# Sixteen more tokens by gathered rows: a dense expert product of 368 columns in place of 384

## The chip, the cores and the metric

The kernel runs on one core of one Trainium2 chip. The metric is the device time of one execution in microseconds, and lower is better. Engines are named as in the profile: PE (TensorE matmul), PEld (its weight loads), DVE (VectorE), ACT (ScalarE), POOL (GpSimd), and SP, which only issues DMAs.

## The reference

One encoder layer over 512 tokens of width 2048. Token mixers come first. What matters here is the last part, a product-key expert layer: each token picks 8 x 16 = 128 of 16384 single-neuron experts, each with a gate, and the output is

```
a   = u_sel . x                      # first expert product
hid = gelu(a) * gate
out = sum over the 128 experts of hid * v_sel   # second expert product
x   = x + out ; out = rmsnorm(x) * g_final
```

## The kernel before

Tokens lie on the free dimension, 512 columns. The first expert product is dense: gelu(u x) for all 16384 experts is written to a DRAM scratch, `act_dram` (128 tiles of 128 experts x 512 tokens). The second product is done in two ways at once in the last stage, the value stage.

**Dense part, 384 tokens (`TD`).** POOL scatter-adds the gates of these tokens into `gates_dram` (L705). The value stage runs over 16 sub-blocks `s` of eight tiles, and each sub-block over 16 output tiles `x`. One (s, x) is called a half here: 256 halves. A half takes one 512 KB piece of `w_v` in a ring of four slots. ACT rounds it (`round_half`, L752: `w_hi`), POOL subtracts (L738: `w_lo`), and PE does 8 x 3 matmuls with `TD` columns (L2079 to L2081): hi x hi, hi x lo, lo x hi. SP loads a slot again once its `w_lo` is made, ACT rounds once PE is done with the half four earlier. DVE adds the result into `yv` (L2053). For eight of the 16 tiles (`PREPARED_AT` = 0, 2, 4, ... 12, 13) the engines also prepare the operand of the next sub-block: DVE multiplies gelu by gate (`product`, L1996), ACT rounds it (`hidden`, L1189) and issues the next loads, DVE subtracts (`low_part`, L2000). ACT does `hidden` ahead of the `round_half` of the same x.

**Gathered part, the last 128 tokens.** One token per partition. For each of its 128 experts POOL issues an indirect DMA that gathers 128 gelu values (`gather_act`, L720) and one that gathers 128 rows of `v_rows`, 1 MB (`gather_row`, L730). DVE multiplies the row by the token's factor and adds it to `y_sparse` in four PSUM banks (`add_row`, L2032). Three row buffers (`ROW_BUFS`). In sub-block 15 ACT copies the sums out, PE turns them (L2459), and DVE adds them to `yv` (L2049).

**The order is written out by hand.** POOL's value loop has a step q for each half: `w_lo` of half q+4, then what `GATHERS[q]` holds. DVE adds the rows of step q at half q+3 (`ROW_LAG`), behind the add of that half and ahead of the product of the next. Before the change, steps 1 to 32 have one act gather each, and from 33 on two steps of every three have an act gather (up to step 175) and, from 36 to 226, the same two of three have a row gather.

## Time and profile before

| what | us |
|---|---|
| median of 3 runs (4304.68 to 4309.94) | 4307.83 |
| profiled execution, its own time | 4316.3 |
| its span | 4314.5 |
| PE busy | 4238.6 |
| POOL busy | 2527.8 |
| DVE busy | 2519.5 |
| ACT busy | 1573.2 |

Matmuls overlap, so PE's busy time says that it had work and not how fast it went; the spacing of matmuls comes from counting them in a window. Idle time in brackets stands in front of an instruction, with what ended it. POOL's row for an indirect DMA is the time in which it makes the DMA, not the transfer. "issue" is time that no wait in the profile explains.

### The profile page before, as it was taken

The page shows a single profiled execution, that of the slowest core. Times are in us where ns is not written, and L with a number is a line of the kernel's source. Part 1 is how long each engine was busy: PE and PEld are TensorE (multiplying, and loading weights), DVE is VectorE, ACT ScalarE, POOL GpSimd, SP SyncE. Part 2 cuts the span into 40 slices and gives each one's busy share as a digit, 9 for nine tenths or more (in the row PEclk, how much of TensorE's full clock was granted, in tenths as well). Part 3 has the DMA queues.
Part 4 walks back from the last instruction along what each step waited for, and adds up shares of the span by engine and source line. Part 5 has one row for each costly group of instructions (what it writes and reads, how often), then busy time and mean ns, then how long its engine had stood idle before and what let it go on. Part 6 is the DMA issues. An engine that isn't in the chain of part 4 may idle for free.

```text
span 4314.5 us, 67486 instructions
## 1 busy us (share of the span) xinstructions
PE 4238.6 (98%) x24940; PEld 3881.5 (90%) x24940; DVE 2519.5 (58%) x3662; ACT 1573.2 (36%) x2079; POOL 2527.8 (59%) x1276
## 2 busy tenths in 40 slices
PE   7999999999999999999999999999989999999998
PEld 6888888888887877888899999999989999999998
DVE  5422443445545433896577777777762477777655
ACT  5222333333334433222444444444443333322332
POOL 5333344443443444444588888887018888888774
PEclk9999999999999999999999999999999999999999
DMA  6696566666667873233355555555465899999983
GB/s 246 198 386 184 153 209 190 186 190 187 183 197 235 268 223 119 93 100 121 113 129 133 125 136 132 129 132 129 137 208 178 282 331 337 333 337 335 356 299 112
DMA packets 574119, 870.50 MB, mean 202 GB/s; under 512 B 85648, under 2 KB 423952, under 8 KB 556944
## 3 DMA queue, kind: packets, MB, share of 16 engines
q1 hardware_dynamic: 401536, 591.47, 43.1%
q0 software_dynamic: 77824, 134.52, 11.8%
q10 hardware_dynamic: 94608, 142.52, 9.3%
q8 instruction: 92, 1.51, 0.1%
q14 instruction: 59, 0.48, 0.0%
HBM read 784.55 MB, written 218.04 MB: 232 GB/s over the span
## 4 chain that ended last, share of the span: by engine, by line
PE 75%; issue 10%; POOL 8%; DMA 3%; DVE 2%; ACT 1%; ACTq 0%; POOLq 0%; DVEq 0%; SPq 0%
PE banks L2079 17%; PE banks L2081 17%; PE banks L2080 17%; PE banks L2416 7%; PE banks L2417 7%; PE banks L2415 7%; POOL w_lo L682 4%; POOL w_lo L738 3%; DMA arena<-expert_rows_scratch,constants 2%; POOL constants L720 1%; PE banks L2280 1%; POOL arena L730 1%; DVE arena L1393 0%; DMA constants<-gelu_scratch 0%; PE banks L2375 0%
## 5 line engine op out<-in xcount | busy, mean ns | idle before, releaser
L2079 PE MATMUL banks<-x_hi,w_hi 128*128 128x512 f32 (+1 forms) x4800 | 1776.4, 370 | 32.4 <-DVE x_lo L2000 15.8
L2080 PE MATMUL banks<-x_lo,w_hi 128*128 128x512 f32 (+2 forms) x4928 | 1798.1, 365 | 0.0
L2081 PE MATMUL banks<-x_hi,w_lo 128*128 128x512 f32 (+1 forms) x4800 | 1761.2, 367 | 0.0
L682 POOL TENSOR_TENSOR w_lo<-w_raw,w_hi 128x1024 fp32r<-128x1024 f32 x364 | 898.7, 2471 | 1425.2 <-ACT w_hi L752 1222.4
L2079 PEld LDWEIGHTS banks<-x_hi,w_hi 128*128 128x128 f32 x4800 | 904.9, 189 | 147.1 <-DVE x_lo L2000 13.3
L2080 PEld LDWEIGHTS banks<-x_lo,w_hi 128*128 128x128 f32 x4928 | 931.5, 189 | 104.4 <-issue 1.2
L752 ACT ACTIVATE w_hi<-w_raw 128x1024 fp32r<-128x1024 f32 x612 | 643.4, 1058 | 1015.2 <-PE banks L2081 909.1
L2081 PEld LDWEIGHTS banks<-x_hi,w_lo 128*128 128x128 f32 x4800 | 904.4, 188 | 108.9
L705 POOL DMA_INDIRECT gate_matrix_scratch<-arena,constants x384 | 741.4, 1931 | 116.9 <-issue 116.9
L738 POOL TENSOR_TENSOR w_lo<-w_raw,w_hi 128x1024 fp32r<-128x1024 f32 x252 | 609.0, 2426 | 142.2 <-ACT w_hi L752 137.9
L2417 PE MATMUL banks<-x_hi,w_lo 128*128 128x256 f32 x1664 | 470.8, 283 | 0.0
L2416 PE MATMUL banks<-x_lo,w_hi 128*128 128x256 f32 x1664 | 470.7, 283 | 0.0
L2415 PE MATMUL banks<-x_hi,w_hi 128*128 128x256 f32 x1664 | 470.6, 283 | 0.0
L2032 DVE SCALAR_TENSOR_TENSOR banks<-arena,constants,banks 128x2048 f32<-128x2048 f32 x127 | 298.8, 2353 | 142.3 <-DMA arena<-expert_rows_scratch,constants 136.0
L2417 PE MATMUL banks<-t_hi,w_lo 128*128 128x256 f32 x1248 | 350.4, 281 | 0.0
L2415 PE MATMUL banks<-t_hi,w_hi 128*128 128x256 f32 x1248 | 350.1, 281 | 0.0
L2416 PE MATMUL banks<-t_lo,w_hi 128*128 128x256 f32 x1248 | 349.9, 280 | 0.0
L2416 PEld LDWEIGHTS banks<-x_lo,w_hi 128*128 128x128 f32 x1664 | 316.2, 190 | 0.0
L2417 PEld LDWEIGHTS banks<-x_hi,w_lo 128*128 128x128 f32 x1664 | 316.2, 190 | 0.0
L2415 PEld LDWEIGHTS banks<-x_hi,w_hi 128*128 128x128 f32 x1664 | 316.0, 190 | 0.0
L2053 DVE TENSOR_TENSOR arena<-arena,banks 128x384 f32<-128x384 f32 x256 | 139.6, 549 | 245.6 <-PE banks L2081 201.2
L1927 DVE TENSOR_TENSOR w_lo<-w_raw,w_hi 128x1024 fp32r<-128x1024 f32 x156 | 190.3, 1220 | 81.3 <-ACT w_hi L1149 81.2
(291 smaller groups left out, 4546.9 us busy)
## 6 DMA issues: line engine op xcount, KB each, us to landing
expert_rows_scratch<-w_v SPq DMA_DIRECT2D x256, 512.0 KB, 5.1
w_raw<-w_u SPq DMA_DIRECT2D x256, 512.0 KB
w_raw<-w_v SPq DMA_DIRECT2D x256, 512.0 KB
w_raw<-w_in SPq DMA_DIRECT2D x200, 512.0 KB
gelu_scratch<-arena ACTq DMA_DIRECT2D x126, 256.0 KB
gate_matrix_scratch<-early_mix_or_one_hots SPq DMA_DIRECT2D x16, 1536.0 KB, 9.6
constants<-gelu_scratch ACTq DMA_DIRECT2D x128, 192.0 KB
early_mix_or_one_hots<-gate_matrix_scratch ACTq DMA_DIRECT2D x32, 768.0 KB
```

What stands on the lines that cost most here:

```text
L682: nc.gpsimd.tensor_tensor(wlo[s][:], raw[s][:], whi[s][:], ALU.subtract).then_inc(w_lo_made, 1)
L705: nc.gpsimd.indirect_dma_start(gate_values, bass.IndirectOffsetOnAxis(gate_index[:, tt, e:e + 1], 0), sel[:, 2, tt, e:e + 1], None, comput ...
L738: nc.gpsimd.tensor_tensor(wlo[m % 4][:], raw[m % 4][:], whi[m % 4][:], ALU.subtract)\
L752: A.activation(whi[s][:], raw[s][:], ACT.Copy).then_inc(w_hi_made, 1)
L1927: V.tensor_tensor(wlo[s][:], operand_source(name), whi[s][:], ALU.subtract).then_inc(pair_lo, 1)
L2032: V.scalar_tensor_tensor(y_sparse, rows[:, e % ROW_BUFS], hid_sparse[:, e:e + 1], y_sparse, ALU.mult, ALU.add).then_inc(rows_added, 1)
L2079: M.matmul(out, whi[s][:, k], h, start=f, stop=False)
L2080: M.matmul(out, whi[s][:, k], l, start=False, stop=False)
L2081: ins = M.matmul(out, wlo[s][:, k], h, start=False, stop=e)
L2415: M.matmul(out, whi[s][:, k], h, start=k == 0, stop=False)
L2416: M.matmul(out, whi[s][:, k], l, start=False, stop=False)
L2417: ins = M.matmul(out, wlo[s][:, k], h, start=False, stop=k == HT - 1)
```

## The change

Sixteen of the 384 dense tokens (the last of them) move to the gathered way. As they are few, each gets eight partitions: partition 8t+g handles 16 of token t's 128 experts. So 16 more act gathers and 16 more row gathers (`E_SLOTS`) are issued, and go through the same row buffers and the same `y_sparse` ahead of the other tokens. DVE then copies the sums to SBUF (`extra_sums`), and PE adds the eight partitions of each token by 16 small products with `group_ones` in sub-block 14. Index values are spread over the partitions through a small DRAM scratch, by DMAs from POOL ahead of the value stage. Dense operands, matmuls, loads and adds have 368 columns (`TV`). Act gathers are now in three of four steps (12 to 181), row gathers in two of three (13 to 227), in blocks of 16 (`HID_BLOCK`) for the factors.

```diff
@@ -70,9 +70,13 @@
 TD = T - P
+EXTRA = 16
+TV = TD - EXTRA
+E_GROUPS = P // EXTRA
+E_SLOTS = P // E_GROUPS
 TG = TD // P
 NE = NK * NK
-HID_BLOCK = 32
+HID_BLOCK = 16
 ROW_BUFS = 3
@@ -162,10 +166,12 @@
     at = {}
+    for j in range(E_SLOTS):
+        at.setdefault((2 * j) // 3, []).append(("extra_act", j))
     for e in range(P):
-        at.setdefault(1 + e if e < HID_BLOCK else 33 + (3 * (e - HID_BLOCK)) // 2, []).append(("act", e))
-    for e in range(P):
-        at.setdefault(36 + (3 * e) // 2, []).append(("row", e))
+        at.setdefault(12 + (4 * e) // 3, []).append(("act", e))
+    for n in range(E_SLOTS + P):
+        at.setdefault(13 + (3 * n) // 2, []).append(("row", n))
     return at
@@ -262,6 +268,7 @@
         v_rows = dram("expert_rows_scratch", [NE, D])
+        extra_dram = dram("extra_tokens_scratch", [3, EXTRA, P])
 
@@ -346,6 +353,12 @@
         rows_added = sem("rows_added")
+        extra_out = sem("extra_tokens_out")
+        extra_in = sem("extra_tokens_in")
+        extra_act_in = sem("extra_act_in")
+        extra_hid = sem("extra_hid")
+        extra_saved = sem("extra_sums_saved")
+        extra_turned = sem("extra_sums_turned")
         sparse_saved = sem("sparse_saved")
@@ -550,6 +563,13 @@
         gate_index = tab[:, 4 * TD + 5 * P:4 * TD + (5 + TG) * P].bitcast(U32).rearrange("p (a b) -> p a b", a=TG)
+        per_extra = tab[:, 4 * TD + (5 + TG) * P:4 * TD + (5 + TG) * P + 6 * EXTRA]\
+            .rearrange("p (k j) -> p k j", j=EXTRA)
+        extra_index, extra_act_index = (per_extra[:, k].bitcast(U32) for k in range(2))
+        extra_gate, extra_act, extra_hidden, group_ones = (per_extra[:, k] for k in range(2, 6))
+        extra_numbers = lmask[:].rearrange("p a b -> p (a b)")[:, 0:2 * P].bitcast(U32).rearrange("p (a b) -> p a b", a=2)
+        extra_sums = [early_a[:].rearrange("p a b -> p (a b)"), eg.rearrange("p a b -> p (a b)")]
+        extra_turns = [bank[2 + h][:, TD:T].rearrange("p (k t) -> p k t", t=EXTRA) for h in range(2)]
         gate_place = sw.rearrange("p a b c -> p (a b c)")[:, 0:TG * P].rearrange("p (a b) -> p a b", a=TG)
@@ -708,28 +728,43 @@
                 add_gate(tt, e)
+            last_tokens = slice(P - EXTRA, P)
+            for k, v in enumerate((extra_numbers[last_tokens, 0], extra_numbers[last_tokens, 1])):
+                pool.dma_start(extra_dram[k].bitcast(U32), v).then_inc(extra_out, 16)
+            pool.dma_start(extra_dram[2], sel[last_tokens, 2, TG - 1]).then_inc(extra_out, 16)
+            pool.wait_ge(extra_out, 48)
+            by_group = extra_dram.rearrange("k t (g j) -> (t g) k j", j=E_SLOTS)
+            pool.dma_start(per_extra[:, 0:3], by_group).then_inc(extra_in, 16)
             low_halves(2 * C_V, 2 * C_V + 4)
...
             act_values = act_dram.rearrange("j i (t o) -> (j i t) o", o=1)
+
+            def gather_extra_act(j):
+                if j == 0:
+                    pool.wait_ge(extra_in, 16)
+                    for b in range(2):
+                        pool.wait_ge(gelu_out[b], 16 * (NK // 2) + 16)
+                nc.gpsimd.indirect_dma_start(extra_act[:, j:j + 1], None, act_values,
+                                             bass.IndirectOffsetOnAxis(extra_act_index[:, j:j + 1], 0))\
+                    .then_inc(extra_act_in, 16)
 
...
                     pool.wait_ge(sparse_index, N_INDEX)
-                    for b in range(2):
-                        pool.wait_ge(gelu_out[b], 16 * (NK // 2) + 16)
                 nc.gpsimd.indirect_dma_start(act_sparse[:, e:e + 1], None, act_values,
...
 
-            def gather_row(e):
-                if e == 0:
+            def gather_row(n):
+                if n == 0:
                     for b in range(4):
                         pool.wait_ge(v_moved[b], 16 * (2 * NK // 4))
-                if e >= ROW_BUFS:
-                    pool.wait_ge(rows_added, e - ROW_BUFS + 1)
-                nc.gpsimd.indirect_dma_start(rows[:, e % ROW_BUFS], None, v_rows,
-                                             bass.IndirectOffsetOnAxis(v_index[:, e:e + 1], 0))\
-                    .then_inc(rows_in[e % ROW_BUFS], 16)
+                if n >= ROW_BUFS:
+                    pool.wait_ge(rows_added, n - ROW_BUFS + 1)
+                e = n - E_SLOTS
+                index = extra_index[:, n:n + 1] if e < 0 else v_index[:, e:e + 1]
+                nc.gpsimd.indirect_dma_start(rows[:, n % ROW_BUFS], None, v_rows, bass.IndirectOffsetOnAxis(index, 0))\
+                    .then_inc(rows_in[n % ROW_BUFS], 16)
 
@@ -738,7 +773,7 @@
                 for what, e in GATHERS.get(q, []):
-                    (gather_act if what == "act" else gather_row)(e)
+                    {"act": gather_act, "extra_act": gather_extra_act, "row": gather_row}[what](e)
 
@@ -1177,16 +1212,16 @@
             def load_gates(s, r):
-                act.dma_start(gsb[:, r], gates_dram[bass.ds(8 * s + 4 * r, 4)].rearrange("j p t -> p j t"))\
+                act.dma_start(gsb[:, r, :, 0:TV], gates_dram[bass.ds(8 * s + 4 * r, 4)][:, :, 0:TV].rearrange("j p t -> p j t"))\
                     .then_inc(gates_read[r], 16)
...
             def load_gelu(s, k):
-                act.dma_start(agb[:, k % 4], act_dram[8 * s + k, :, 0:TD]).then_inc(gelu_in[k % 4], 16)
+                act.dma_start(agb[:, k % 4, 0:TV], act_dram[8 * s + k, :, 0:TV]).then_inc(gelu_in[k % 4], 16)
 
...
                 act.wait_ge(hid_product, 8 * s + (k + 1))
-                A.activation(xhi[:, 8 * half + k, 0:TD], htmp[:, k % 2], ACT.Copy).then_inc(hid_hi, 1)
+                A.activation(xhi[:, 8 * half + k, 0:TV], htmp[:, k % 2, 0:TV], ACT.Copy).then_inc(hid_hi, 1)
 
@@ -1296,7 +1331,7 @@
                         if x == 0:
-                            act.wait_ge(rows_added, P)
+                            act.wait_ge(rows_added, E_SLOTS + P)
                             for c in range(4):
@@ -1846,10 +1881,14 @@
                                                  ALU.mult, ALU.add))
+            V.tensor_copy(extra_numbers[:, 0], gate_place[:, TG - 1])
+            V.tensor_scalar(extra_numbers[:, 1], gate_place[:, TG - 1], float(T), small[:, 68 + TG - 1:69 + TG - 1],
+                            ALU.mult, ALU.add)
             for t in range(TG):
...
             index_step(10, V.tensor_copy(gate_index, gate_place))
+            V.reduce_sum(group_ones, ident.rearrange("p (t g) -> p t g", g=E_GROUPS), AX_X)
             index_step(11, V.tensor_scalar(small[:, 78:79], small[:, 79:80], float(TD), None, ALU.add))
@@ -1989,15 +2028,17 @@
             def product(s, k):
+                if isinstance(s, int) and s == 0 and k == 0:
+                    dve.wait_ge(extra_out, 48)
                 dve.wait_ge(gates_read[k // 4], 16 * s + 16)
...
                     dve.wait_ge(hid_lo, 8 * s + (k - 1))
-                V.tensor_tensor(htmp[:, k % 2], agb[:, k % 4], gsb[:, k // 4, k % 4], ALU.mult).then_inc(hid_product, 1)
+                V.tensor_tensor(htmp[:, k % 2, 0:TV], agb[:, k % 4, 0:TV], gsb[:, k // 4, k % 4, 0:TV], ALU.mult).then_inc(hid_product, 1)
 
...
                 dve.wait_ge(hid_hi, 8 * s + (k + 1))
-                V.tensor_tensor(xlo[:, 8 * half + k, 0:TD], htmp[:, k % 2], xhi[:, 8 * half + k, 0:TD], ALU.subtract)\
+                V.tensor_tensor(xlo[:, 8 * half + k, 0:TV], htmp[:, k % 2, 0:TV], xhi[:, 8 * half + k, 0:TV], ALU.subtract)\
                     .then_inc(hid_lo, 1)
@@ -2017,20 +2058,31 @@
 
-            def add_row(e):
-                dve.wait_ge(rows_in[e % ROW_BUFS], 16 * (e // ROW_BUFS) + 16)
-                if e % HID_BLOCK == 0:
+            def add_row(n):
+                dve.wait_ge(rows_in[n % ROW_BUFS], 16 * (n // ROW_BUFS) + 16)
+                e = n - E_SLOTS
+                if n == 0:
+                    dve.wait_ge(extra_act_in, 16 * E_SLOTS)
+                    V.tensor_tensor(extra_hidden, extra_act, extra_gate, ALU.mult).then_inc(extra_hid, 1)
+                    dve.wait_ge(extra_hid, 1)
+                if n == E_SLOTS:
+                    dve.wait_ge(rows_added, n)
+                    for h in range(2):
+                        V.tensor_copy(extra_sums[h], y_sparse[:, h * HW:h * HW + HW]).then_inc(extra_saved, 1)
+                    dve.wait_ge(extra_saved, 2)
+                if e >= 0 and e % HID_BLOCK == 0:
                     block = slice(e, e + HID_BLOCK)
...
                     dve.wait_ge(sparse_index, N_INDEX + 1 + e // HID_BLOCK)
-                if e == 0:
-                    V.tensor_scalar(y_sparse, rows[:, 0], hid_sparse[:, 0:1], None, ALU.mult).then_inc(rows_added, 1)
+                hid = extra_hidden[:, n:n + 1] if e < 0 else hid_sparse[:, e:e + 1]
+                if n == 0 or e == 0:
+                    V.tensor_scalar(y_sparse, rows[:, n % ROW_BUFS], hid, None, ALU.mult).then_inc(rows_added, 1)
                 else:
-                    dve.wait_ge(rows_added, e)
-                    V.scalar_tensor_tensor(y_sparse, rows[:, e % ROW_BUFS], hid_sparse[:, e:e + 1], y_sparse,
-                                           ALU.mult, ALU.add).then_inc(rows_added, 1)
+                    dve.wait_ge(rows_added, n)
+                    V.scalar_tensor_tensor(y_sparse, rows[:, n % ROW_BUFS], hid, y_sparse, ALU.mult, ALU.add)\
+                        .then_inc(rows_added, 1)
 
@@ -2050,7 +2102,11 @@
                         dve.wait_ge(sparse_saved, 5)
-                    V.tensor_tensor(yv[:, x, 0:TD], yv[:, x, 0:TD], bank[x % 4][:, 0:TD], ALU.add).then_inc(y_added, 1)
+                    if s == 14 and x in (2, 3):
+                        dve.wait_ge(extra_turned, x - 1)
+                        extra = yv[:, HT * (x - 2):HT * (x - 2) + HT, TV:TD]
+                        V.tensor_tensor(extra, extra, extra_turns[x - 2], ALU.add)
+                    V.tensor_tensor(yv[:, x, 0:TV], yv[:, x, 0:TV], bank[x % 4][:, 0:TV], ALU.add).then_inc(y_added, 1)
                     if s < 15 and x - 1 in PREPARED_AT:
@@ -2458,8 +2514,14 @@
                         ins.then_inc(sparse_turned, 1)
+                    if isinstance(s, int) and s == 14 and x in (2, 3):
+                        pe.wait_ge(extra_saved, 2)
+                        for k in range(HT):
+                            ins = M.matmul(extra_turns[x - 2][:, k], extra_sums[x - 2][:, P * k:P * k + P], group_ones,
+                                           start=True, stop=True)
+                        ins.then_inc(extra_turned, 1)
                     m = KT * s + (2 * C_V + x)
-                    half(m, (2 * C_V + x) % 4, bank[x % 4][:, 0:TD], list(range(8)), 8 * par, True, True, width=TD,
+                    half(m, (2 * C_V + x) % 4, bank[x % 4][:, 0:TV], list(range(8)), 8 * par, True, True, width=TV,
                          ready=(lambda k: pe.wait_ge(hid_lo, k + 1)) if first and x == 0 else None)\
```

## Rows read from the trace of the kernel before

**Rows 1.** page, the span in 40 slices (busy tenths of PE, POOL and DMA)
```profile
PE   7999999999999999999999999999989999999998
...
POOL 5333344443443444444588888887018888888774
...
DMA  6696566666667873233355555555465899999983
```
**Rows 2.** windows: us, busy (xinstructions) PE, PEld, DVE, ACT, POOL; PEclk, DMA share, GB/s
```profile
2000.00:2050.00 50.00, 50.00 (x223) 41.39 (x222) 16.77 (x38) 11.81 (x14) 22.79 (x10) 1.00 0.38 121
2300.00:2350.00 50.00, 50.00 (x422) 50.00 (x421) 37.81 (x38) 22.50 (x28) 43.00 (x24) 1.00 0.58 137
3700.00:3750.00 50.00, 50.00 (x290) 50.00 (x289) 36.96 (x31) 14.62 (x17) 43.35 (x28) 1.00 0.92 317
```
**Rows 3.** the same view, three stretches of the value stage
```profile
3250.00:3370.00 120.00, 120.00 (x694) 120.00 (x693) 29.78 (x59) 38.05 (x43) 98.84 (x58) 1.00 0.58 174
3370.00:3970.00 600.00, 595.29 (x3414) 594.35 (x3413) 419.25 (x377) 181.16 (x210) 530.07 (x328) 0.99 0.94 332
3970.00:4180.00 210.00, 210.00 (x1213) 210.00 (x1212) 139.57 (x139) 68.78 (x79) 162.81 (x87) 1.00 0.94 349
```
**Rows 4.** groups of instructions, window 3370 to 3970 us
```profile
L738 POOL TENSOR_TENSOR w_lo<-w_raw,w_hi 128x1024 fp32r<-128x1024 f32 x141 | 338.0, 2411 | 27.5 <-ACT w_hi L752 23.6 <-issue 2.2
...
L2032 DVE SCALAR_TENSOR_TENSOR banks<-arena,constants,banks 128x2048 f32<-128x2048 f32 x91 | 214.1, 2353 | 130.8 <-DMA arena<-expert_rows_scratch,constants 124.8 <-issue 6.0
...
L720 POOL DMA_INDIRECT constants<-gelu_scratch,constants x94 | 101.5, 1079 | 14.6 <-issue 11.5
L730 POOL DMA_INDIRECT arena<-expert_rows_scratch,constants x93 | 90.6, 974 | 28.3 <-issue 28.3
L2000 DVE TENSOR_TENSOR x_lo<-level_masks,x_hi 128x384 fp32r<-128x384 f32 x70 | 78.9, 1127 | 0.0
...
L1996 DVE TENSOR_TENSOR level_masks<-constants,early_mix_or_one_hots 128x384 f32<-128x384 f32 x71 | 68.1, 959 | 0.0
```
**Rows 5.** groups of instructions, windows 3230 to 3370, then 3970 to 4180 us
```profile
L738 POOL TENSOR_TENSOR w_lo<-w_raw,w_hi 128x1024 fp32r<-128x1024 f32 x35 | 85.7, 2448 | 30.5 <-ACT w_hi L752 30.4
...
L720 POOL DMA_INDIRECT constants<-gelu_scratch,constants x34 | 33.3, 980 | 5.1 <-issue 2.2
...
L730 POOL DMA_INDIRECT arena<-expert_rows_scratch,constants x35 | 36.6, 1047 | 5.3 <-issue 1.2 <-DVE banks L2032 0.2
```
**Rows 6.** timeline of POOL: start us, us, instruction
```profile
3229.00 4.77 POOL L738 TENSOR_TENSOR w_lo<-w_raw,w_hi 128x1024 fp32r<-128x1024 f32 x2 [14.17 <-ACT w_hi L752]
...
3596.23 2.41 POOL L738 TENSOR_TENSOR w_lo<-w_raw,w_hi 128x1024 fp32r<-128x1024 f32 x1
...
3601.23 4.77 POOL L738 TENSOR_TENSOR w_lo<-w_raw,w_hi 128x1024 fp32r<-128x1024 f32 x2
...
3630.34 2.41 POOL L738 TENSOR_TENSOR w_lo<-w_raw,w_hi 128x1024 fp32r<-128x1024 f32 x1 [2.30 <-ACT w_hi L752]
```
**Rows 7.** chain that ended last: start us, us, piece
```profile
3612.52 11.57 DMA arena<-expert_rows_scratch,constants
...
3671.37 7.12 DMA arena<-expert_rows_scratch,constants
```
**Rows 8.** timeline of PE, then of DVE, near 3688, 4234 and 4294 us
```profile
3687.90 0.44 PE L2079 MATMUL banks<-x_hi,w_hi 128*128 128x384 f32 x1 [2.23 <-DVE x_lo L2000]
...
3689.09 0.52 PE L2080 MATMUL banks<-x_lo,w_hi 128*128 128x384 f32 x1
...
4234.31 1.91 PE L2459 MATMUL banks<-constants,arena 128*128 128x128 f32 x16
...
4294.52 0.55 DVE L2053 TENSOR_TENSOR arena<-arena,banks 128x384 f32<-128x384 f32 x1 [2.22 <-PE banks L2081]
```
**Rows 9.** idle of DVE and of POOL before the value stage
```profile
2143.57 7.13 DVE L1894 TENSOR_TENSOR t_lo<-arena,t_hi 128x2048 fp32r<-128x2048 f32 x3 [40.30 <-ACT t_hi L1167]
...
L682 POOL TENSOR_TENSOR w_lo<-w_raw,w_hi 128x1024 fp32r<-128x1024 f32 x1 | 2.4, 2405 | 193.1 <-ACT w_hi L1201 193.1
```

## The prediction

> **What bounds the kernel now.** I began with the slices of the page [rows 1]: PE is busy in nine tenths nearly throughout, so elsewhere only PE's work could matter. The change touches the last quarter alone, and there POOL's digits rise to 8 and DMA's to 9. Three resources are near full at once, and the question is which of them is left over when PE gets shorter.
>
> PE's price is read from windows without a stall [rows 2]: 50 us hold 223 matmuls of 512 columns, 422 of 256, 290 of 384, so one takes 224.2, 118.5 and 172.4 ns. From 256 to 384 columns that is 0.42 ns a column, from 384 to 512 0.40. A half of 24 matmuls with 384 columns takes 4.138 us.
>
> POOL's price comes from the groups in the 600 us where both kinds of gather run [rows 4]. `w_lo`: (338.0 + 27.5 - 23.6)/141 = 2.425 us, its wait for ACT taken off. An act gather: (101.5 + 14.6)/94 = 1.235. A row gather: (90.6 + 28.3)/93 = 1.278. With 94 and 93 gathers to 141 steps a step costs 576.9/141 = 4.09 us. POOL is thus 96% taken; only the 23.6 us of waiting for ACT's `w_hi` is room. PE needs 4.14. What was reached is 600/141 = 4.255. The missing 0.1 us are waits between engines: the timeline shows PE stopped for 2.23 us for `x_lo` at 3687.90, after which matmuls come 0.3 us apart in place of 0.17 for some 4 us [rows 8].
>
> The third is the transfer of rows. In this stretch the DMA engines are busy 94% [rows 3], DVE waits 124.8 us for rows [rows 4], and the chain of waits holds pieces of 7.12 and 11.57 us from gather to landing [rows 7].
>
> **What the change takes away.** At 368 columns a matmul takes 172.4 - 16 x 0.42 = 165.7 ns, a half 3.977 us, 0.161 less. Were PE the only bound, 256 halves would give 41.2 us. The 16 extra tokens also take 1/24 off each gate and gelu load and off DVE's three operations of a half; DVE and ACT have room, so I count nothing.
>
> **What it adds to POOL.** 32 gathers. In steps 13 to 181 there are 127 act and 113 row gathers in 169 steps. At the prices above: 169 x 2.425 + 127 x 1.235 + 113 x 1.278 = 409.8 + 156.8 + 144.4 = 711.0 us, 4.21 a step. This is over PE's 3.977: here POOL becomes the bound and PE waits for `w_lo`. A gather that stands alone in its step is cheaper: 1.13 for act, 1.20 for a row, with `w_lo` at 2.448 [rows 5]. About 85 of the steps hold both kinds, so 42 acts and 28 rows stand alone: 4.4 and 2.2 us less, and 84 x 0.02 more for `w_lo`: 706. Bounds: 692.5 with all gathers at the lone prices, 711 at the paired ones.
>
> The end is reckoned on this path. POOL starts its steps at 3229.0 [rows 6], set by the end of the stage before. Steps 0 to 12 hold 17 act gathers: 13 x 2.448 + 17 x 1.13 = 51.0; with 3.92 a step POOL just keeps up with PE. Then 706, and 2.4 for the `w_lo` of half 186: 3988.4. From there steps have rows alone, 2.45 + 0.8 = 3.25, below PE, so 70 halves at 3.977 follow: 278.4. In the last sub-blocks PE turns sums in 1.9 us [rows 8]; the 16 small products are not in the trace. Between 0 and the 1.9 us that 16 transposes of 128 columns take, I use 1.9. End of the last half: 3988.4 + 278.4 + 3.8 = 4270.6, against 4294.5 now [rows 8]. The gain is 23.9 us before any waits between engines.
>
> **Other edits.** The two copies of 1024 columns out of PSUM are half a row addition each (2.35 us for 2048 [rows 4]): together 2.4 us in DVE's order at half 40, behind which the next product and so ACT wait. Bounds 0 and 2.4; I take 2.4, as that stretch has no room. The 16 row additions are 37.6 us of DVE; they lie mostly in halves 16 to 39, where DVE now is a quarter busy (29.8 of 120 us [rows 3]). They cost nothing; without that cover DVE would be the bound for them. The small index operations on DVE lie ahead of an idle of 40.3 us, POOL's four small DMAs with their wait in an idle of 193.1 us [rows 9]; even at 2 us each they vanish. The two adds and the extra waits in sub-block 14 find their inputs made 180 halves before. Rows now start at step 13 where DMA is 58% busy [rows 3]: room for 16.8 MB.
>
> **The waits between engines.** This is the term that decides. ACT's `w_hi` of half q+4 stands behind `hidden`, that behind DVE's product, that behind the row of POOL's step q-4. So POOL's step q may start only when that row has landed and was added: three steps, 12.6 us, must hold landing, 2.35 for the addition, at least 0.55 for the product, and ACT's two operations of about 0.5 and 1.06. With gaps some 5 us beside the landing, so a landing over about 7.5 us stops POOL; 7.12 just passes, 11.57 was followed by a wait of 2.30 at 3630.34 [rows 6, 7]. Products and low parts average 0.96 and 1.13 us against 0.55 undisturbed, being held while POOL subtracts: with two `w_lo` in a row, 4.77 us, the hold is longest [rows 4, 6]. Today 23.6 us of such waits fall on 141 steps, a part of them harmless because PE was ahead. Carried whole to 169 steps that is 28.3; none at all is 0. For the change speaks that a step with no gather, and so the pair of `w_lo`, comes once in 12 and no more once in 3, and that the three steps between row and `w_lo` grow: 3 x 2.425 + 2 x 1.278 and 2 acts, 12.3 us, become the same with 2.25 acts, 12.6. Against it: DMA stays full, and POOL now has no faster partner to hide a wait behind. I take 12, between the ends.
>
> Gain: 23.9 - 2.4 - 12 = 9.5 us. The terms are of the profiled execution (its own time 4316.3, 8.5 above the median); taken off the median, 4307.8 - 9.5 = 4298.3.
>
> **Rivals.** *No waits.* If every landing stays below 7.5 us, the gain is 23.9 - 2.4 = 21.5 us: 4286. For it: 7.12 passed; against it: 11.57 [rows 7]. The Trainium skill, "DMA: Bandwidth & Descriptors", section "Anatomy of one DMA", fits a transfer made by POOL as 2.0 us plus bytes over 436 GB/s, an estimate of 4.4 us for 1 MB; both rows are longer, and by that rule this rival would be sure.
>
> *Waits recur whole (20 to 28 us).* Then the gain is 21.5 - 28.3 = -6.8 to 1.5 us: no measurable change, 4306 to 4315. For it: the DMA share stays where it is. Against: fewer pairs.
>
> *Landing becomes the bound (slower).* One mechanism: with a step at 4.2 us DMA is as full as now, and if in each of the 10.6 sub-blocks of the bound stretch one more landing reaches 11.6 us, each costs 11.6 - 7.5 = 4 us on top of 12 - gain 21.5 - 12 - 42 = -33, 4340. It decides from about 18 us more, that is at two in five of them (slower by 8.6). Half of them gives 4319. Against: a share below 1, and the rows-only stretch runs at 94% too, with PE never stopped [rows 3].
>
> *PE's whole gain.* If POOL's gathers had room to shrink (waiting inside them), 41.2 us and the stalls of today: 4260. A step would have to fall below 3.98; at the lone prices it is still 692.5/169 = 4.10. So hardly.
>
> *The clock.* A stall of 2.23 us was followed by matmuls 0.3 us apart, the lower of the two clock levels, 1.2 GHz [rows 8]. If PE, now waiting in most halves, stays low, a half takes 24 x 0.32 = 7.7 us and PE is the bound again at once; ten more such stretches of 12 matmuls cost 18 us where POOL's lead does not absorb them, and the time would be 4316. The Trainium skill, "TensorE: Matmul & The Clock Gate", section "HAM oscillation — how this bites in real kernels", describes a kernel whose waits lower the clock again and again. Against it: the waits here are 0.2 us a half on average and 1 us behind a step with both gathers, not 2.23; but before, PE hardly waits, so the trace can't exclude it.
>
> **Numbers.** Within 0.2%, 8.6 us, this kernel can't be told from no change. Gathers bind and part of the waits goes (up to 4299): 0.33; no waits: 0.10. Waits recur (4299 to 4316): 0.32. Landing 0.15, clock 0.05 (both slower, 4316 up). Whole gain 0.05 and below 4284. Faster 0.48, same 0.32, slower 0.20. The low end: lone prices (13.5 us less) with 12 of waits give 4285; the high end is 4319 with half of the landings late. Range 4284 to 4319; the likeliest case alone 4284 to 4299.
>
> **What would show it.** In windows of the changed kernel from 3300 to 3950: matmul spacing 165.7 ns when PE runs freely; a POOL step of 4.17 to 4.21 us besides its waits for ACT's `w_hi`, these about 12 us in sum; PE waiting for POOL's `w_lo` in many halves, some 35 to 45 us in sum (169 steps of 4.18 against 3.977, and the 12); the last `w_lo` of the bound stretch near 3988 plus waits; end of the last half near 4285. Wrong if POOL's waits for `w_hi` reach 28 us, if gathers take clearly less than 1.23, or if the granted clock falls below 0.97 in the stretch.

## The result and the profile after

| | us |
|---|---|
| after, median of 4 runs (4332.72 to 4338.06) | 4335.41 |
| before, median of 4 runs beside them (4304.68 to 4309.94) | 4308.24 |
| after : before | 1.0063, 95% interval 1.0051 to 1.0076 |
| profiled execution of after, its own time (span) | 4335.65 (4333.9) |

The changed kernel is slower by 27 us. The forecast was a gain of 9.5 us, 4298.3, with 4284 to 4319 as the range: the sign and the range were both missed.

The slices of the page after, POOL and DMA, beside [rows 1]:

```profile
POOL 5333344434443444444688888886038888888874
...
DMA  7695566666667873233355555555368999999983
```

Windows of after: the stretches of [rows 3], and one of 50 us to compare with [rows 2].

```profile
3250.00:3370.00 120.00, 114.63 (x672) 113.07 (x672) 83.14 (x70) 35.59 (x43) 106.71 (x67) 0.99 0.83 283
3370.00:3970.00 600.00, 565.28 (x3293) 555.01 (x3292) 469.69 (x371) 171.73 (x204) 522.61 (x330) 0.99 0.91 320
3970.00:4180.00 210.00, 205.50 (x1216) 204.69 (x1216) 154.40 (x142) 67.47 (x79) 173.12 (x98) 0.98 0.95 352
```
```profile
3500.00:3550.00 50.00, 50.00 (x302) 50.00 (x301) 40.38 (x31) 13.68 (x16) 43.22 (x28) 1.00 0.90 313
```

In the last one 50/302 gives 165.6 ns a matmul, as forecast (165.7). But the 600 us hold 3293 of these shorter matmuls, and 3414 of the longer ones before. PE was idle for 34.7 us of them, not 4.7. POOL was less busy than before as well (522.6 against 530.1), and so was DMA (0.91 against 0.94). Nothing became fuller, so the engines waited for one another.

Groups of after in the same 600 us, beside [rows 4]:

```profile
L773 POOL TENSOR_TENSOR w_lo<-w_raw,w_hi 128x1024 fp32r<-128x1024 f32 x136 | 326.6, 2405 | 37.1 <-ACT w_hi L787 35.1 <-issue 0.2
...
L754 POOL DMA_INDIRECT constants<-gelu_scratch,constants x103 | 107.9, 1048 | 16.1 <-issue 13.0
L2041 DVE TENSOR_TENSOR x_lo<-level_masks,x_hi 128x368 fp32r<-128x368 f32 x68 | 104.9, 1543 | 0.0
L766 POOL DMA_INDIRECT arena<-expert_rows_scratch,constants x91 | 89.2, 980 | 24.4 <-issue 24.4
L2037 DVE TENSOR_TENSOR level_masks<-constants,early_mix_or_one_hots 128x368 f32<-128x368 f32 x68 | 86.7, 1275 | 0.0
```

POOL's prices, worked out as in the prediction: `w_lo` (326.6 + 37.1 - 35.1)/136 = 2.416 us, an act gather 124.0/103 = 1.204, a row gather 113.6/91 = 1.248. For steps 13 to 181 that makes 169 x 2.416 + 127 x 1.204 + 113 x 1.248 = 702.2 us, 4.16 a step, against the 706 forecast. The time they really took is read from POOL's timeline:

```profile
3225.56 2.42 POOL L773 TENSOR_TENSOR w_lo<-w_raw,w_hi 128x1024 fp32r<-128x1024 f32 x1 [13.39 <-ACT w_hi L787]
...
3277.94 2.41 POOL L773 TENSOR_TENSOR w_lo<-w_raw,w_hi 128x1024 fp32r<-128x1024 f32 x1
...
4023.12 2.41 POOL L773 TENSOR_TENSOR w_lo<-w_raw,w_hi 128x1024 fp32r<-128x1024 f32 x1 [0.26 <-ACT w_hi L787]
```

The three lines open the steps 0, 13 and 182. So the 169 steps from 13 to 181 took 745.2 us, 4.41 each. POOL's own work is 702.2 of them; 43.0 us is waiting. The view of waits for this stretch agrees: 42.5 us for `w_hi`, in 38 waits. It follows here from 3300 to 3980 us, before first, then after, then a kernel that comes below (the kernel before with the new order of gathers alone). The numbers are us in total, times, and the longest.

```profile
POOL w_lo L738 <- ACT w_hi L752: 35.1, 39, 3.2
...
PEld banks L2079 <- POOL w_lo L738: 5.7, 3, 2.5
PE banks L2079 <- DVE x_lo L2000: 4.7, 3, 2.2
```
```profile
PEld banks L2135 <- POOL w_lo L773: 45.8, 34, 4.7
POOL w_lo L773 <- ACT w_hi L787: 40.0, 35, 2.5
PE banks L2135 <- DVE x_lo L2041: 27.6, 9, 4.4
```
```profile
POOL w_lo L738 <- ACT w_hi L752: 49.4, 51, 2.5
...
PEld banks L2079 <- POOL w_lo L738: 22.0, 12, 4.5
...
PE banks L2079 <- DVE x_lo L2000: 18.1, 7, 4.2
```

POOL's wait for `w_hi` is 40.0 us in these 680, where the forecast took 12 for its 169 steps. The lines of PEld and PE show largely the same stops, seen by the weight load and by the matmul, so they must not be added. The loop behind one such wait can be read in the timeline of after, DVE first, then ACT, then POOL:

```profile
3504.95 2.36 DVE L2084 SCALAR_TENSOR_TENSOR banks<-arena,constants,banks 128x2048 f32<-128x2048 f32 x1
...
3507.66 2.43 DVE L2041 TENSOR_TENSOR x_lo<-level_masks,x_hi 128x368 fp32r<-128x368 f32 x1
3510.01 2.34 DVE L2084 SCALAR_TENSOR_TENSOR banks<-arena,constants,banks 128x2048 f32<-128x2048 f32 x1
3512.28 0.53 DVE L2037 TENSOR_TENSOR level_masks<-constants,early_mix_or_one_hots 128x368 f32<-128x368 f32 x1
```
```profile
3512.84 0.51 ACT L1224 ACTIVATE x_hi<-level_masks 128x368 fp32r<-128x368 f32 x1 [8.89 <-DVE level_masks L2037]
...
3513.54 2.01 ACT L787 ACTIVATE w_hi<-w_raw 128x1024 fp32r<-128x1024 f32 x2 [0.19 <-issue]
```
```profile
3507.27 2.41 POOL L773 TENSOR_TENSOR w_lo<-w_raw,w_hi 128x1024 fp32r<-128x1024 f32 x1
...
3514.68 2.41 POOL L773 TENSOR_TENSOR w_lo<-w_raw,w_hi 128x1024 fp32r<-128x1024 f32 x1 [2.49 <-ACT w_hi L787]
```

DVE adds a row at 3504.95. (Ahead of that row it waited 2.62 us for the landing and then made the factors of a block of 16, an operation that took 2.88 us.) DVE's low part starts at 3507.66, just after POOL's subtraction (3507.27), and takes 2.43 us where an undisturbed one takes 0.53: it ends 0.41 us after POOL's. The second row follows, and only at 3512.28 the product for which ACT has been waiting 8.89 us. ACT's `w_hi` stands behind that, and POOL, two gathers later, waits 2.49 us for it. So two things lie in this loop: DVE's order (row ahead of product) and DVE being held. PE is busy throughout these 50 us: one such pass does not yet stop it.

### The profile page after: what moved, and what is told of

It reads as the page before. It is cut to its first block, busy times and chain, and to the rows that moved or that the text cites. A ratio compares the mean times of both kernels' runs of the same rounds, so it can differ in the third digit from the quotient of the medians.

```text
span 4333.9 us, 67635 instructions
## 1 busy us (share of the span) xinstructions
PE 4219.0 (97%) x24972; PEld 3852.0 (89%) x24972; DVE 2665.1 (61%) x3690; ACT 1567.1 (36%) x2079; POOL 2561.7 (59%) x1312
## 4 chain that ended last, share of the span: by engine, by line
PE 70%; issue 11%; POOL 9%; DMA 5%; DVE 3%; ACT 1%; ACTq 0%; POOLq 0%; DVEq 0%; SPq 0%
PE banks L2135 15%; PE banks L2137 15%; PE banks L2136 15%; PE banks L2472 7%; PE banks L2473 7%; PE banks L2471 7%; DMA arena<-expert_rows_scratch,constants 4%; POOL w_lo L773 4%; POOL w_lo L702 4%; POOL constants L754 1%; PE banks L2336 1%; DVE level_masks L2037 1%; ACT w_hi L787 1%; POOL arena L766 0%; DMA w_raw<-w_u 0%
## 5 line engine op out<-in xcount | busy, mean ns | idle before, releaser
L2084 DVE SCALAR_TENSOR_TENSOR banks<-arena,constants,banks 128x2048 f32<-128x2048 f32 x142 | 334.1, 2353 | 151.1 <-DMA arena<-expert_rows_scratch,constants 145.7
L1224 ACT ACTIVATE x_hi<-level_masks 128x368 fp32r<-128x368 f32 x128 | 65.3, 511 | 579.3 <-DVE level_masks L2037 542.7
```

The source lines that it names most:

```text
L2084: V.scalar_tensor_tensor(y_sparse, rows[:, n % ROW_BUFS], hid, y_sparse, ALU.mult, ALU.add)\
```

## The experiments

Theories. **Loop:** the row's landing and addition stand ahead of the product on DVE, and so ahead of ACT's `w_hi` and POOL's `w_lo`; the new order of gathers makes this loop longer. **Hold:** DVE's product and low part are stretched while POOL subtracts; PE is then stopped at the start of a sub-block, for which the low parts come too late. **Work:** POOL is simply over its limit through the 32 added gathers.

### Which part of the change costs the time

The new order of the gathers alone, in the kernel before (no added tokens, 384 columns), and then the blocks of 16 alone:

```diff
-HID_BLOCK = 32
+HID_BLOCK = 16
-        at.setdefault(1 + e if e < HID_BLOCK else 33 + (3 * (e - HID_BLOCK)) // 2, []).append(("act", e))
+        at.setdefault(12 + (4 * e) // 3, []).append(("act", e))
-        at.setdefault(36 + (3 * e) // 2, []).append(("row", e))
+        at.setdefault(37 + (3 * e) // 2, []).append(("row", e))
```

> The kernel before with the new order alone: act gathers in three of four steps from 12, row gathers in two of three from 37, factors in blocks of 16; no extra tokens, 384 columns. If the order (gathers that mostly fall apart, a row's loop that meets other steps, twice the small factor products) costs by itself: 4320 or more. If only the rate of gathers and the narrower product matter: within 6 us of 4308; POOL's step 4.13 there is under PE's 4.14.

Measured: 4338.46 us, 1.0071 (1.0054 to 1.0087), 30 us slower than before (4308.72).

```diff
-HID_BLOCK = 32
+HID_BLOCK = 16
-        at.setdefault(1 + e if e < HID_BLOCK else 33 + (3 * (e - HID_BLOCK)) // 2, []).append(("act", e))
+        at.setdefault(1 + e if e < 32 else 33 + (3 * (e - 32)) // 2, []).append(("act", e))
```

> The kernel before with the factors of the gathered experts in blocks of 16 in place of 32, the order of its gathers kept. Theory E: eight small products, each held for some 2.5 us with a wait of about 2.5 us for the row in front, in place of four: 4 x 5 = 20 us, 4328. Theory D: within 4 us of 4308.

Measured: 4308.60, 0.9999 (0.9990 to 1.0009). In the old order the blocks cost nothing, so the 30 us come with the new order. (The new order with blocks of 32 was not run, so that the blocks cost something only there is not excluded.) The waits shown above say how: POOL's wait for `w_hi` grows from 35.1 to 49.4 us and PE's stops for `x_lo` from 4.7 to 18.1. The same 680 us, before and with the order alone:

```profile
3300.00:3980.00 680.00, 675.29 (x3875) 674.35 (x3874) 444.09 (x417) 208.44 (x241) 595.62 (x367) 0.99 0.90 315
```
```profile
3300.00:3980.00 680.00, 660.66 (x3756) 656.51 (x3755) 479.53 (x410) 202.00 (x235) 586.09 (x364) 0.99 0.87 304
```

PE does 119 matmuls fewer, 20.5 us at 172.4 ns; 14.6 us of that is PE standing still, the rest slower matmuls behind the stops. Not one gather was added for that.

The changed kernel with matmuls of 384 columns (the last 16 columns are computed and dropped):

```diff
-                    half(m, (2 * C_V + x) % 4, bank[x % 4][:, 0:TV], list(range(8)), 8 * par, True, True, width=TV,
+                    half(m, (2 * C_V + x) % 4, bank[x % 4][:, 0:TD], list(range(8)), 8 * par, True, True, width=TD,
```

> The changed kernel with matmuls of 384 columns again (16 columns of each product are worked out and thrown away), all else with 368. Theories A, B and C: in the stretch with both gathers PE isn't the bound, so 0.161 us a half is lost only in the 87 halves outside: about 14 us, 4349. If PE's own time is the bound throughout: 256 x 0.161 = 41 us, 4376.

Measured: 4347.72, 1.0094 (1.0077 to 1.0111): 12 us slower than after. And the other way round, the kernel before with 368 dense columns (the second product of the sixteen tokens is left out):

```diff
+TV = TD - 16
-                V.tensor_tensor(htmp[:, k % 2], agb[:, k % 4], gsb[:, k // 4, k % 4], ALU.mult)
+                V.tensor_tensor(htmp[:, k % 2, 0:TV], agb[:, k % 4, 0:TV], gsb[:, k // 4, k % 4, 0:TV], ALU.mult)
...
-                    half(m, (2 * C_V + x) % 4, bank[x % 4][:, 0:TD], list(range(8)), 8 * par, True, True, width=TD,
+                    half(m, (2 * C_V + x) % 4, bank[x % 4][:, 0:TV], list(range(8)), 8 * par, True, True, width=TV,
```

> The kernel before with 368 dense columns and nothing in their place (the gathered part of sixteen tokens is left out): what the narrower product is worth with the old order. If PE were the bound, 41 us less, 4267. With POOL at 4.09 a step in the stretch of both gathers and PE at 3.977 elsewhere: 143 steps gain 0 to 0.05 us, 113 halves 0.161, 18 to 25 us, 4287.

Measured: 4291.00 beside 4310.84, 0.9951 (0.9934 to 0.9967). Even with no gather added, narrower matmuls are worth 20 us here and not the 41 of PE's own work.

One sum follows from four kernels: order alone 4338.46 - 4308.72 = +30; the added gathers and the rest at 384 columns 4347.72 - 4338.46 = +9; narrowing 4335.41 - 4347.72 = -12. Together +27, the result. The shares depend on the path, though. By way of the old order they are: narrowing alone 4291.00 - 4310.84 = -20; then the added gathers and the rest with a paired order like the old one (4315.12, `a_pairs` below) +24; then the new order +20. (That is 25 in sum and not 27, as the kernel before took 4310.84 beside the first of them.) So **Work** is 9 us where the order already makes the engines wait, but 24 us where it does not: there the added gathers use up all that the narrower product gives. The order decides the sign; without it the change would still have gained nothing.

### Cutting the loop

DVE makes the product of the next tile ahead of the row additions of its half:

```diff
-                    if s < 15 and x in PREPARED_AT:
-                        product(s + 1, PREPARED_AT.index(x))
+                    if s < 15 and x == 0:
+                        product(s + 1, 0)
...
+                    if s < 15 and x + 1 in PREPARED_AT:
+                        product(s + 1, PREPARED_AT.index(x + 1))
                     for e in rows_added_at(q):
                         add_row(e)
```

> The changed kernel with one thing moved: DVE makes the product for the next tile ahead of the row additions of this tile, not behind them. Theory A (a loop: POOL's w_lo waits for ACT's w_hi, that for the product, that for a row that POOL issued four steps earlier to land): the loop is cut, POOL's waits for w_hi in the stretch with both gathers fall from 43 us to under 15, and the median from 4335 to about 4305. Theory B (DVE's SBUF operations are held while POOL subtracts, and this alone makes them late): the holds stay, 4325 or more. Theory C (DMA is full and rows simply come late): 4330 or more.

Measured: 4311.12, 1.0005 (0.9995 to 1.0014), 24 us faster than after. The second way gives each row one more step to land:

```diff
-ROW_LAG = 3
+ROW_LAG = 4
```

> The changed kernel with ROW_LAG 4 in place of 3: DVE adds a row one half later, so that the loop from gather to w_lo has four POOL steps in place of three. Theory A: a landing of up to 11 us passes, about 4310. Theory B: no change, about 4335. Theory C: DVE waits less for rows but the rate of rows is the same, about 4335.

Measured: 4315.93, 1.0017 (1.0007 to 1.0026), 19 us faster than after. The group of `w_lo`, window 3370 to 3970, with the product ahead and then with lag 4:

```profile
L773 POOL TENSOR_TENSOR w_lo<-w_raw,w_hi 128x1024 fp32r<-128x1024 f32 x143 | 344.0, 2410 | 10.9 <-ACT w_hi L787 8.1
```
```profile
L773 POOL TENSOR_TENSOR w_lo<-w_raw,w_hi 128x1024 fp32r<-128x1024 f32 x140 | 336.6, 2408 | 15.8 <-ACT w_hi L787 13.5
```

The wait for `w_hi` falls from 35.1 to 8.1 and 13.5 us, and 143 and 140 halves fit into the window in place of 136. Two different edits of the same loop give nearly the same gain, so the **loop** is shown. Both are slightly short of the forecasts (4305 and 4310), and in both ACT now waits for the DMA that loads `w_raw`, 34.0 and 31.3 us in the window, against 0.2 in after. Now the order: act gathers in the same two of three steps as rows, in the changed kernel, and then with lag 4.

```diff
-        at.setdefault(12 + (4 * e) // 3, []).append(("act", e))
+        at.setdefault(13 + (3 * e) // 2, []).append(("act", e))
```

> The changed kernel with act gathers in the same two of three steps as the row gathers (13 to 203), not in three of four. Theory D (what costs is an order in which steps with one gather, both or none follow unevenly against the even tiles that are prepared): the order of before is restored, the loss of 30 us that the order alone showed is undone, about 4305. Theory E (the order costs through its rows or its small factor products in blocks of 16, not through where the act gathers stand): 4325 or more.

> The changed kernel with paired gathers and ROW_LAG 4. If a row's landing is what is left of POOL's waiting (28 us in a_pairs): 4300. If DVE's held operations at the end of a sub-block take its place, as with the product ahead: 4315 or more.

Measured: 4315.12, 1.0017 (1.0007 to 1.0026), 20 us faster than after with the same gathers; with lag 4 4319.11, 1.0028 (1.0017 to 1.0040). The two cures don't add up. With pairs or lag the kernel is still 6 to 7 us behind before; with the product ahead, before's time is reached.

### The hold

If the loop were all, the product ahead of the rows should help the kernel before as well, and the paired order.

> The kernel before with the product for the next tile ahead of the row additions. Theory A: its 24 us of POOL waiting for w_hi and the two PE stops of some 4 us each mostly go; PE at 4.138 us a half is then the bound: 4298. If the loop binds only where POOL is over PE's time: within 4 us of 4308.

> Both mends in the changed kernel: product ahead of the row additions, act gathers in the steps of the rows. If both act on the same waits they don't add: as the better of the two, about 4303. If they are separate: 4290. POOL's own work bounds it from below: 190 steps of 4.09 us and the rest at 3.977 give about 4283.

Measured: the kernel before with that edit 4329.86, 1.0052 (1.0036 to 1.0069), so 21 us slower; the changed kernel with pairs and that edit 4331.76, 1.0058 (1.0041 to 1.0075). Both expectations failed. The timeline of the kernel before with the product ahead, at the start of a sub-block: DVE, POOL, then PE.

```profile
3690.59 4.55 DVE L2000 TENSOR_TENSOR x_lo<-level_masks,x_hi 128x384 fp32r<-128x384 f32 x1
3695.06 0.54 DVE L2053 TENSOR_TENSOR arena<-arena,banks 128x384 f32<-128x384 f32 x1
```
```profile
3690.04 4.67 POOL L738 TENSOR_TENSOR w_lo<-w_raw,w_hi 128x1024 fp32r<-128x1024 f32 x2
...
3703.53 2.39 POOL L738 TENSOR_TENSOR w_lo<-w_raw,w_hi 128x1024 fp32r<-128x1024 f32 x1 [6.29 <-ACT w_hi L752]
```
```profile
3695.27 0.68 PE L2081 MATMUL banks<-x_hi,w_hi 128*128 128x384 f32 x1 [4.30 <-DVE x_lo L2000]
3695.75 0.53 PE L2082 MATMUL banks<-x_lo,w_hi 128*128 128x384 f32 x1
```
```profile
3690.00:3695.20 5.20, 0.97 (x6) 0.65 (x4) 5.20 (x4) 1.06 (x1) 5.03 (x4) 0.90 1.02 416
3695.30:3702.00 6.70, 6.70 (x23) 6.70 (x24) 3.03 (x3) 0.52 (x1) 1.63 (x2) 0.57 0.88 307
```

DVE's low part starts inside a pair of `w_lo`, is held until both are done, and takes 4.55 us. PE stops for it for 4.30 us, then runs at a granted clock of 0.57 of 2.4 GHz, that is mostly at 1.2, in the 6.7 us that follow. ACT can't round before PE is done, and POOL waits 6.29 us. It is a chain of its own, once per sub-block. It should go when the operand is finished earlier:

```diff
-PREPARED_AT = [0, 2, 4, 6, 8, 10, 12, 13]
+PREPARED_AT = [0, 2, 4, 6, 7, 8, 10, 11]
```

> The changed kernel with the operand of the next sub-block prepared at tiles 0, 2, 4, 6, 7, 8, 10, 11 in place of 0, 2, 4, 6, 8, 10, 12, 13. Theory F (what costs are PE's stops at the start of a sub-block, for a low_part that DVE makes late at the end of the one before): the stops go and with them their 28 us and the lower clock behind them, 4305. Theory A: the products still stand behind rows, 4330 or more.

Measured: 4334.77, 1.0060 (1.0043 to 1.0076). PE's stops for `x_lo` are gone (0 us from 3370 to 3970), yet the time hasn't moved: POOL still waits 32.8 us for `w_hi` in the window, and other waits have come up, here in the same window:

```profile
ACT w_hi L787 <- DMA w_raw<-w_v: 43.9, 8, 7.7
...
PE banks L2135 <- POOL w_lo L773: 30.7, 39, 2.3
```

After had 0.2 us of the first and 10.5 of the second. PE stands still nearly as long as in after (32.6 us against 34.7), only for another reason. So this run doesn't show that the stops for `x_lo` cost nothing; it shows that removing them alone brings nothing. With the product ahead, early tiles were then set beside it, in the kernel before, in after, and in after with pairs:

> The kernel before with the product ahead and the early tiles. G: the three stops of b_late (POOL waiting 6.3 us each, PE 4.3 and then at 0.32 us a matmul) go, PE at 4.138 a half is the bound: about 4299. If not G: 4320 or more.

> The changed kernel with the product ahead of the row additions and the operand prepared at tiles 0, 2, 4, 6, 7, 8, 10, 11. Two mechanisms (G): the first is cut by the product ahead, PE's stops at the start of a sub-block (16.6 us in a_late) by the early tiles; POOL's own work is left: 169 steps at 4.14 and 87 halves at 3.977, about 4302 against 4311 in a_late. One mechanism (A alone): as a_late, 4311. If the weights' own DMA becomes late, as in a_early: 4325 or more.

> The same with act gathers in the steps of the rows. G: PE's stops of 4 to 9 us in a_late_pairs go, and POOL at 4.05 a step is left: 4331 falls to about 4290. If the product ahead is bad for the paired order for another reason: 4320 or more.

Measured: 4309.48 (1.0001, 0.9991 to 1.0010), 4307.69 (0.9998, 0.9988 to 1.0007) and 4312.01 (1.0004, 0.9995 to 1.0014). Where the product ahead had cost 21 us (the kernel before) and 17 us (after with pairs), early tiles give 20 back in each. In after with the product ahead they change little: 4307.69 against 4311.12. So there are two ways in which PE is stopped, and an edit that hits only one can make the other worse.

The hold by itself: the kernel before in the new order, its product buffer moved to PSUM, where POOL here reads nothing. To free two banks, each row is added in two operations of 1024 columns into the same sums (half of the row sums are lost), and a control does only that.

```diff
-                V.tensor_tensor(htmp[:, k % 2], agb[:, k % 4], gsb[:, k // 4, k % 4], ALU.mult)
+                V.tensor_tensor((htmp if isinstance(s, int) and s == 0 else hps)[:, k % 2, 0:TD], agb[:, k % 4], gsb[:, k // 4, k % 4], ALU.mult)
...
-                V.tensor_tensor(xlo[:, 8 * half + k, 0:TD], htmp[:, k % 2], xhi
+                V.tensor_tensor(xlo[:, 8 * half + k, 0:TD], (htmp if isinstance(s, int) and s == 0 else hps)[:, k % 2, 0:TD], xhi
...
+        hps = psum[:, 6:8]
```

> Control for the run b_psum: the kernel before with the new order, and each row added in two operations of 1024 columns into the same 1024 sums (the sums of the gathered tokens are meaningless). Both theories: as the order alone, 4338, within 8 us; somewhat more as DVE pays the fixed part of an operation twice.

> As b_two, but the product of gelu and gate is written to the two PSUM banks that this frees, so that low_part has one SBUF input in place of two; the saved sums read banks 4 and 5 twice (the sums of the gathered tokens are meaningless). Theory B (DVE's operations with two SBUF inputs are held until POOL's subtraction ends): low_part falls from over 1.2 us to about 0.55 and the time by 10 us or more against b_two, with fewer PE stops for x_lo. Theory A (row landing ahead of the product in DVE's order): low_part isn't in the loop, within 4 us of b_two.

Measured: control 4339.50, 1.0067 (1.0051 to 1.0084); PSUM 4332.27, 1.0051 (1.0034 to 1.0068), 7 us less, where the theory of the hold had forecast 10 or more and its rival 4 at most. The low part in the control and with PSUM, window 3300 to 3980:

```profile
L2001 DVE TENSOR_TENSOR x_lo<-level_masks,x_hi 128x384 fp32r<-128x384 f32 x78 | 99.2, 1271 | 0.0
```
```profile
L2002 DVE TENSOR_TENSOR x_lo<-banks,x_hi 128x384 fp32r<-128x384 f32 x79 | 43.4, 550 | 0.0
```

With one of its inputs in PSUM it takes its undisturbed 550 ns, the longest of the 79 560 ns. The product, whose inputs both stay in SBUF, gets longer (1315 against 1063 ns in the same windows). The hold is shown. Taking it off the low part is worth 7 us net of the longer product; the hold of the product was not taken away.

### A version that beats both

If POOL is what is left, some of its work should go to DVE. In the changed kernel with product ahead and early tiles, DVE makes `w_lo` for one half in 16, then for two (12 and 24 halves of 192). The cut shows the second.

```diff
+BY_DVE = [q for q in range(16, 208) if q % 16 in [5, 13]]
...
-                if m < HALVES:
+                if m < HALVES and q not in BY_DVE:
...
+                    if q in BY_DVE:
+                        m = 2 * C_V + 4 + q
+                        dve.wait_ge(w_hi_made, m + 1)
+                        dve.wait_ge(w_lo_made, m)
+                        V.tensor_tensor(wlo[m % 4][:], raw[m % 4][:], whi[m % 4][:], ALU.subtract).then_inc(w_lo_made, 1)
```

> a_late_early with the w_lo of one half in 16 made by DVE (12 halves from 16 to 207, at the thirteenth tile). If POOL's own work is the bound: 12 x 2.42 = 29 us off POOL, a step of 3.99 on average, 4280 to 4285, the first version faster than the kernel before. If the waits between engines take its place (DVE's subtraction is itself held and stands in the row's loop): 4300 or more.

> The same with two halves in 16 (24 of them). If POOL's own work is the bound: a step of 3.84, below PE's 3.977, so only 0.16 us a step are gained in 169 steps: 4280. If the waits take its place: no better than a_dve1 or worse.

Measured: 4298.57, 0.9972 (0.9961 to 0.9984), and 4288.98 beside 4309.97, 0.9953 (0.9936 to 0.9970). The second is 46 us faster than after and 21 faster than before. Its window and DVE's own subtraction:

```profile
3370.00:3970.00 600.00, 590.86 (x3508) 583.58 (x3508) 498.53 (x416) 184.45 (x218) 526.94 (x334) 1.00 0.95 344
```
```profile
L2119 DVE TENSOR_TENSOR w_lo<-w_raw,w_hi 128x1024 fp32r<-128x1024 f32 x19 | 23.2, 1219 | 23.0 <-POOL w_lo L776 23.0
```

3508 matmuls in 600 us, against 3293 in after and 3414 before. DVE needs 1.22 us for what costs POOL 2.42, and 12 halves moved gave 9 us, the next 12 gave 10: 0.8 us each. That is a third of the POOL time moved; had POOL's work been the only bound, the first 12 halves would have given up to 29 us (4280 to 4285), and the second run was forecast at 4280. So POOL's work limits this version in part, and waits between engines take the rest. Moving halves in the kernel before was not run, so how much of the 21 us needs the narrower product is open.

## Why the prediction was wrong

The terms in the order of the prediction, in the profiled execution:

| step | forecast | measured |
|---|---|---|
| matmul of 368 columns | 165.7 ns | 165.6 |
| POOL's first step | 3229.0 | 3225.6 |
| steps 0 to 12 | 51.0 us | 52.4 |
| POOL's own work, steps 13 to 181 | 706 us | 702.2 |
| waits in them | 12 (0 to 28.3) | 43.0 |
| the two copies in DVE's order | 2.4 (0 to 2.4) | within the waits |
| from there to the end of the last half | 284.6 | 290.9 |
| last half ends | near 4285 | 4314.0 |
| granted clock in the stretch | over 0.97 | 0.99 |

DVE's last add of a half, of after:

```profile
4314.04 0.54 DVE L2109 TENSOR_TENSOR arena<-arena,banks 128x368 f32<-128x368 f32 x1 [2.07 <-PE banks L2137]
```

**The step that failed is "The waits between engines".** POOL's own work in these steps came out within 1%. The waits were 43.0 us and not 12, outside even the bound of 28.3, which was before's 23.6 carried on by the number of steps. That step said of itself that it decides, and it held that the new order would make the waits fewer, as pairs of `w_lo` come once in 12 steps. The pairs did get fewer, 9 in the 600 us against 36 before. But DVE was held more often: of the low parts, 25 of 68 took 2 us or longer after, 20 of 68 with the order alone, and 11 of 70 before. The order by itself costs 30 us. The fault was to count pairs and mean step lengths for a loop of which single passes decide, with the product in that loop put at its undisturbed 0.55 us. PE's stops were misplaced with it. The forecast had 35 to 45 us of waiting for `w_lo` in many halves; in these steps PE waited 12.7 us for `w_lo` and 31.5 us for `x_lo`, in ten stops, about one a sub-block.

**The second fault is that before's slack was counted as gain.** The 23.9 us set a sum without any waits (4.18 a step) beside a time of before that has its waits in it (4.255). Of such waits only 12 us were then charged. Before's 0.1 us a step were waits of the same kind, and no run of the changed kernel without relief for POOL got clearly under before's time (best 4307.69). With POOL's own work at 4.16 a step and PE's former half at 4.138, the narrower product has nothing left to give in these 169 steps; it can only pay behind them.

**The tail** was 6.3 us too short, though PE never stopped in it. At 4023.1 PE had 71.4 halves left (1714 matmuls) and not the 70.6 of the sum. The 16 small products took 3.8 us, twice their upper bound of 1.9: they stand in the trace as 32 matmuls. The two copies took 1.2 us each, as forecast.

**From profile to median.** The sum's own forecast for the profiled execution was 4316.3 - 9.5 = 4306.8, and 4335.65 came: 28.8 off. Before's profiled run lay 8.5 above its median, after's 0.2; taking the gain off the median added these 8 us to the miss.

**The rivals.** *Waits recur whole* named the place rightly, POOL's waits for `w_hi`, with the price at two thirds of what came (28.3 against 43.0). *Landing becomes the bound* had the sign and a chance of 0.15. Its loop is the one that the product ahead and lag 4 cut, but its reason, longer transfers through a fuller DMA, isn't borne out: the DMA share fell to 0.91, and DVE waited 105.5 us for rows in the 600 us, against 124.8 before. What was longer is DVE's part between landing and product. The Trainium skill's page "SBUF — State Buffer", section "SBUF: two separate sides", has a rule for the hold: an operation of DVE with two SBUF inputs and one of GpSimd that reads SBUF exclude each other for the whole instruction. This trace agrees (2.43 us for 0.53, ending 0.41 us after POOL's). The prediction had seen the hold in the averages but priced its loop without it. *No waits* and *PE's whole gain* fell with it. *The clock* did not decide in after.

**Open.** Why this order, with a quarter of the pairs of `w_lo`, lengthens the loop is not settled. In the kernel with the order alone the product rose from 959 [rows 4] to 1283 ns and the low part from 1127 to 1328, so more of them fell under POOL's subtractions; how the 30 us divide between this and the row's place in the loop was not separated. The number of held operations doesn't price it alone: with lag 4, 29 of 70 low parts took 2 us or longer, and the kernel was 19 us faster. In the 600 us, the six factor operations of a block of 16 took 2.6 us each in the kernel with the order alone, where the three of a block of 32 took 0.67 before; their part was not separated either. Nor was what bounds the versions with product ahead and early tiles: ACT waits for `w_raw` loads there, 85.4 us in the 600 us, and 64.5 with 24 halves moved.

## What to carry to other kernels

When several engines pass work round a loop and all stand within a few per cent of their limit, price the waits of one concrete pass of the new order, instruction by instruction, and not the mean step: here the work was right within 1% and the waits off by a factor of more than three. Run a new order alone before adding work in it. And if shortening one engine's work leaves another as the bound, also look for work that can be moved off that other: here 24 halves moved to DVE, at half the price, gave 19 us, about what the narrower product gave with nothing added.

## What was not expected of the hardware

- A DVE operation with both inputs in SBUF is held for the whole of POOL's running subtraction, also over two in a row: 4.55 us for a 0.54 us operation (`b_late`, 3690.59); a multiplication of 16 columns, `constants<-constants`, took 2.88 us at 3502.04 of after. With one input in PSUM it was never lengthened (550 ns on average in 79, 560 at most).
- After one stop of 4.30 us PE's matmuls of 384 columns came 0.32 us apart instead of 0.17, at a granted clock of 0.57 over 6.7 us: 23 matmuls where 39 would fit, 2.7 us beyond the stop itself. Before's stop of 2.23 us [rows 8] was followed by 4.1 us at 0.58. A short stop costs PE more than its length.
- POOL's subtraction of 1024 columns takes 2.41 us, DVE's 1.22 us.
